# The second expert layer in units of 32 tokens, in plain fp32 with four column groups, each expert's weights loaded once

## The reference

```python
def moe(h, w_router, b_router, w1, w3, w2):
    N, D = h.shape                                   # second layer: 512, 1024
    scores = jax.nn.sigmoid(h @ w_router)            # 16 experts in 4 groups of 4
    ...                                              # best group, then its two best experts
    wts = wts / wts.sum(-1, keepdims=True)           # weights of the two
    ...                                              # tokens sorted by expert
    def expert_block(args):
        xb, e = args
        return (jax.nn.silu(xb @ w1[e]) * (xb @ w3[e])) @ w2[e]
    ...
    return jnp.zeros((N, D), h.dtype).at[tok_s].add(out[dest] * w_s[:, None])
```

## Time and profile before

| | us |
|---|---|
| median of three runs | 2587.99 |
| lowest, highest | 2586.57, 2590.0 |
| span of the profiled execution | 2585.1 |
| PE busy | 2436.7 (94%) |
| DVE busy | 1915.5 (74%) |
| ACT busy | 1327.3 (51%) |
| POOL busy | 298.1 (12%) |
| PE's share of the chain that ended last | 89% |

### The profile page before, as it was taken

The page is one execution under the profiler, slowest core; times in us unless marked ns, Lnnn a source line. Parts: engine busy times, 40 slices in busy tenths (PEclk is TensorE's granted clock), DMA queues, the critical chain, the costliest instruction groups (busy, mean ns, idle before and its releaser), DMA issues.

```text
span 2585.1 us, 30193 instructions
## 1 busy us (share of the span) xinstructions
PE 2436.7 (94%) x10883; PEld 1767.2 (68%) x10883; DVE 1915.5 (74%) x2100; ACT 1327.3 (51%) x1280; POOL 298.1 (12%) x330
## 2 busy tenths in 40 slices
PE   6999988996999999999979999999988999999995
PEld 3555534545888888888758887666446888888884
DVE  2899956446888888888857724776357888898887
ACT  3000104115777777777562234465116777777774
POOL 0534411220000000000110002110000000000002
PEclk8999999997999999999979999999988999999998
DMA  9110265439999999999951233125339999999994
GB/s 337 40 66 33 82 252 150 159 139 379 422 422 396 385 388 388 387 387 386 357 213 56 77 117 116 35 87 184 147 147 368 422 401 391 388 388 380 387 387 148
DMA packets 151272, 671.84 MB, mean 260 GB/s; under 512 B 24938, under 2 KB 34410, under 8 KB 94882
## 3 DMA queue, kind: packets, MB, share of 16 engines
q1 hardware_dynamic: 128562, 591.68, 58.9%
q0 software_dynamic: 20208, 74.98, 8.0%
q10 hardware_dynamic: 2432, 4.26, 0.5%
HBM read 612.59 MB, written 58.29 MB: 260 GB/s over the span
## 4 chain that ended last, share of the span: by engine, by line
PE 89%; DVE 3%; DMA 3%; ACT 2%; issue 1%; SPq 1%; POOL 1%; ACTq 0%; DVEq 0%; POOLq 0%
PE ps L826 85%; PE ps L1010 1%; PE ps L1016 1%; ACT arena L1303 1%; DMA arena<-in_w_in_ab_dram 1%; PE ps L914 1%; SPq L411 0%; DMA buf_d<-arena 0%; POOL arena L699 0%; DMA arena<-buf_d,slots 0%; DMA buf_d<-arena,slots 0%; PE ps L1272 0%; DVE arena L1754 0%; DMA arena<-buf_d 0%; DMA arena<-in_w_ada_dram 0%
## 5 line engine op out<-in xcount | busy, mean ns | idle before, releaser
L1864 DVE TENSOR_TENSOR wl<-wx,wh 128x2048 fp32r<-128x2048 f32 x432 | 969.2, 2286 | 49.2 <-ACT wh L1303 49.2
L1303 ACT ACTIVATE wh<-wx 128x2048 fp32r<-128x2048 f32 x432 | 819.4, 1915 | 160.0 <-PE ps L826 143.1
L826 PE MATMUL ps<-wh,xT 128*128 128x512 f32 x2304 | 736.5, 396 | 4.9 <-DVE xT L1881 4.9
L826 PE MATMUL ps<-arena 128*128 128x512 f32 (+5 forms) x2232 | 714.0, 492 | 14.9 <-ACT arena L1303 6.5
L826 PEld LDWEIGHTS ps<-arena 128*128 128x128 f32 (+1 forms) x2232 | 381.2, 188 | 322.4 <-issue 293.2
L826 PEld LDWEIGHTS ps<-wh,xT 128*128 128x128 f32 x2304 | 435.2, 189 | 105.8 <-DVE xT L1881 5.7
L826 PE MATMUL ps<-wl,xT 128*128 128x512 f32 x1152 | 455.1, 395 | 0.0
L826 PE MATMUL ps<-wh,gT 128*128 128x512 f32 x1152 | 378.2, 399 | 0.0
L1303 ACT ACTIVATE arena<-ps 128x512 f32<-128x512 f32 (+7 forms) x231 | 139.6, 619 | 449.3 <-PE ps L826 365.3
L826 PEld LDWEIGHTS ps<-wl,xT 128*128 128x128 f32 x1152 | 217.7, 189 | 47.2
L826 PEld LDWEIGHTS ps<-wh,gT 128*128 128x128 f32 x1152 | 216.8, 188 | 47.3
(11 more groups left out here) (255 smaller groups left out, 2262.9 us busy)
## 6 DMA issues: line engine op xcount, KB each, us to landing
wx<-in_w_dram SPq DMA_DIRECT2D x432, 1024.0 KB, 8.5
arena<-in_w_ada_dram SPq DMA_DIRECT2D x40, 1024.0 KB, 8.3
arena<-buf_d POOLq DMA_DIRECT2D x38, 512.0 KB, 10.7
buf_d<-arena POOLq DMA_DIRECT2D x36, 512.0 KB, 7.8
craw<-in_w_in_c_dram SPq DMA_DIRECT2D x8, 2048.0 KB, 8.6
buf_d<-arena POOLq DMA_DIRECT2D x1, 14848.0 KB, 57.4
arena<-in_w_in_ab_dram SPq DMA_DIRECT2D x8, 1024.0 KB, 12.6
arena<-in_w_out_ab_dram SPq DMA_DIRECT2D x4, 2048.0 KB, 8.0
```

The lines of the kernel that those rows point to most:

```text
L826: return pe.matmul(bank_ap, lhsT, rhs, start=first, stop=last)
L1303: return act.activation(out_, in_, f, **kw)
L1864: v.tensor_tensor(wl[:, g], wx[:, g], whs[g % NH].bitcast(F32), ALU.subtract).then_inc(m["low"], 1)
```

## The change

In the second layer, the buffer of 128-row blocks goes. DRAM gets `h_d` (each token's normalised row, stored by ACT) and `xi_d`, a list of token numbers with room for 768 entries for each expert. `scatter` writes 16-byte entries into `xi_d`. DVE builds a table `utab`: for each unit its expert (`U_E`), its first entry (`U_ROW`); for each expert the units before it (`U_BEF`); and the number of units (`U_N`).

A unit is up to 32 tokens of one expert. POOL reads the unit's 32 entries four times over into `uix` (128 numbers of 4 bytes) and gathers 128 quarter rows of 1 KB into `ux`, so the array's 128 partitions hold 4 quarters by 32 tokens. PE transposes that with two instructions. `sweep` then multiplies in plain fp32: for each of four groups and two slices it sends four products, one for each quarter of 256 output columns, to the four column groups of the array. Three sweeps make a unit: 96 matmuls. The product of gate and value moves from DVE to POOL. ACT stores the result.

The weights take two places. SP loads group `g` of expert `e` into `un_raw[g]` when the copy of expert `e-1` out of it is done. DVE copies it to the fixed place `un_w[g]` when the last unit of expert `e-1` has used that. There is no split into high and low parts, and each expert is loaded once.

```diff
@@ SP
+            def unit_weights(e, groups, later=False):
+                for g in groups:
+                    if later:
+                        sp.wait_ge(un["copied"], e * PAIRS + (g + 1 - PAIRS))
...
+                    sp.dma_start(un_raw[g].rearrange("p k n -> p (k n)").unsqueeze(1), src).then_inc(un["w"][g // 2], 16)
@@ POOL
+                def rows_of(u):
+                    r = pool.value_load(utab[0:1, bass.ds(U_ROW + u, 1)], min_val=0, max_val=NSLOT - UT)
+                    pool.dma_start(uix[:, 0:1], xi_rows[:, bass.ds(r, UT), :], allow_slow_non_contiguous=True).then_inc(un["ix"], 16)
+                def gather_x():
+                    pool.indirect_dma_start(ux, None, h_rows, bass.IndirectOffsetOnAxis(ap=uix[:, 0:1], axis=0)).then_inc(un["xg"], 16)
...
+                with pool.Fori(0, nu) as u:
+                    pool.wait_ge(un["xg"], u * 16 + 32)
+                    rows_of(u + 2)
+                    pool.wait_ge(un["turn"], u * 2 + 2)
+                    pool.wait_ge(un["ix"], u * 16 + 48)
+                    pool.wait_ge(un["hid"], u * 2 + 2)
+                    pool.tensor_tensor(ugg, us0, ugg, ALU.mult).then_inc(un["g"], 1)
+                    gather_x()
@@ PE
+                def sweep(bank, e12, g0, actsT, s):
+                    for g in range(4):
+                        pe.wait_ge(un["copied"], e12 + (g0 + g + 1))
+                        for i in range(2):
+                            for q in range(4):
+                                ins = mm(ps[32 * q:32 * q + 32, bank, 0:256], actsT[:, i * P + 32 * g:i * P + 32 * g + 32],
+                                         un_w[g0 + g][:, i, 256 * q:256 * q + 256], g + i == 0, g + i == 4)
+                        ins.then_inc(s, 1)
+                def place(u):
+                    return pe.value_load(utab[0:1, bass.ds(U_E + u, 1)], min_val=0, max_val=PAIRS * (NX - 1))
...
+                with pe.Fori(1, nu) as u:
+                    gate_up(u, place(u), False)
+                    down(u - 1, place(u - 1))
+                    turn_g(u)
+                down(nu - 1, place(nu - 1))
@@ ACT
+                        if n == 3:
+                            act.wait_ge(h_rdy, j + 1)
+                            act.dma_start(h_d[(t - CT) * P:(t - CT + 1) * P, :], hall[:, t, :]).then_inc(un["h"], 16)
...
+                with act.Fori(1, nu) as u:
+                    silu(u, False)
+                    up(u, False)
+                    turned_x(u + 1)
+                    out_y(u - 1)
+                    turned_g(u)
@@ DVE
+                with v.Fori(0, NX) as e:
+                    c = v.value_load(utab[0:1, bass.ds(U_BEF + e, 1)], min_val=0, max_val=UMAX)
+                    for g in range(PAIRS):
+                        v.wait_ge(un["w"][g // 2], e * 32 + 32)
+                        if g < 8:
+                            v.wait_ge(un["gu"], c * 8 + (g + 1))
+                        else:
+                            v.wait_ge(un["w2"], c * 4 + (g - 7))
+                        v.tensor_copy(un_w[g], un_raw[g]).then_inc(un["copied"], 1)
```

More of the change, by code:

```diff
@@ L58 @@
 FMAX = S // P - 1
+UT = 32
+CAP = S
+NSLOT = NX * CAP
+UMAX = 2 * S_LAT // UT + NX - 1
+U_E, U_ROW, U_BEF, U_N = 0, 64, 128, 144
 EPS = 1e-6
@@ L78 @@
 C_SEL = 600
-C_END = 696
+C_U = 696
+C_END = 698
+C_TOK = C_END + P + NX
 def i_mod32():
@@ L132, in program @@
     buf_v = buf_d.rearrange("(b p) d -> p b d", p=P)
+    h_d = dram("h_d", [S_LAT, D])
+    xi_d = dram("xi_d", [NSLOT, 4], I32)
     es = ExitStack()
@@ L215, in program @@
         ln_pe, ln_dv, ln_act = sems("ln_pe ln_dv ln_act")
[L217 to L221, removed]
+        moe = {s: sem(f"m0_{s}") for s in "used high low xg tx ab si g tg ye yst done".split()}
+        moe["w"] = [sem(f"m0_w{i}") for i in range(PAIRS // 2)]
+        un = {s: sem(f"un_{s}") for s in "gu w2 copied ix xg turn actsT hid g ye yst h".split()}
+        un["w"] = [sem(f"un_in{i}") for i in range(PAIRS // 2)]
         cw, hl_rdy, c_high, c_low, z_use = sems("cw hl_rdy c_high c_low z_use")
@@ L303, in program @@
         geff = at(50480, 2 * KE * NX + NX)
+        un_raw = [at(6144 + 2048 * UNIT_PLACE[g], 2, D) for g in range(PAIRS)]
+        un_w = [at(30720 + 2048 * g if g < 9 else 2048 * (g - 9), 2, D) for g in range(PAIRS)]
+        ux, uxT, us0, ugg, ugT, uy = (at(49152 + 256 * i, 256) for i in range(6))
+        uix = nc.alloc_sbuf_tensor_at("uix", [P, 2], I32, offset=base + 4 * 50688)[:]
+        tokf = at(50696, 4 * NT)
+        tok = nc.alloc_sbuf_tensor_at("tok", [P, NT, 4], I32, offset=base + 4 * 50720)[:]
+        utab = nc.alloc_sbuf_tensor_at("utab", [P, 192], I32, offset=base + 4 * 50744)[:]
+        u_th, u_tt, u_tr = at(48240, NX, NX), at(48496, 4, 32), at(48624, P)
+        h_rows = h_d.rearrange("s (c n) -> (s c) n", c=4)
+        y_rows = buf_d[0:UT * UMAX, :].rearrange("s (c n) -> c s n", c=4)
+        u_sk = at(50936, 2, NT - CT)
+        u_slots = nc.alloc_sbuf_tensor_at("u_slots", [P, 2, NT - CT], I32, offset=base + 4 * 50944)[:]
+        xi_rows = xi_d.rearrange("s (c o) -> c s o", o=1)
         def item_at(n):
@@ L580, in _ @@
             for n in range(16, 24):
-                sp.wait_ge(moe[0]["used"], nb * PAIRS + (n - 16 + 4))
+                sp.wait_ge(moe["used"], nb * PAIRS + (n - 16 + 4))
                 item_load(n)
-            sp.wait_ge(moe[0]["done"], 1)
+            sp.wait_ge(moe["done"], 1)
             chain(2)
@@ L652, in _ @@
             chain(3)
-            sp.wait_ge(moe[1]["xg"], 16)
-            await_stores(sp, 4)
-            expert_weights(1, 0, None, range(6, PAIRS))
+            units()
+            sp.wait_ge(un["copied"], NX * PAIRS)
             sp.wait_ge(u_st[1], stored(10, 1))
@@ L817, in _ @@
             scatter(1)
-            pool.wait_ge(u_mm, 40)
-            experts(1)
+            units()
             gather(4)
```

221 lines of the change are left out of this document (196 added, 25 removed).

## The result

The changed kernel takes 2602.35 us (median of four runs, 2602.12 to 2608.14) against 2588.24 for the kernel before on the same chip. The ratio is 1.0061, with a 95% interval from 1.0047 to 1.0075. It is slower by 0.6%. The forecast was 2575.

A forecast was written before the change was run, and what follows sets the result against it. PE was taken to bound the 602 us stage, with transfers nearly full. Changed stage: 573 plus 13 for GpSimd, 586; with +3 at the start, 2575 us. Range 2530 to 2625, likeliest case 2550 to 2592.

The forecast's parts named there:

- max(units x 12.3, 32.2): Second layer, per expert: the larger of PE's 12.3 us a unit and 32.2 us of loads; sum 597.3 us.
- the same two thirds: Share taken of the lead from loads starting one unit before a PE-bound expert's end: 24 us off 597.3, leaving 573.
- the 13 us for GpSimd: Added to the stage for POOL's product held by DVE's copy bursts: a third of the lower end of 34 to 60.
- Sets in four column groups: PE's sweeps: four matmuls run at once in 0.433 us a set, 24 sets or 10.4 us a unit, 32-wide loads hidden.
- The unit's price: PE's time for one unit: 10.4 + 0.44 + 0.6 + 0.85 = 12.3 us, bounds 11.4 and 13.2.
- the table read: PE's read at the unit loop's head, exposed once a unit because its queue is empty: 0.85 us.
- L = 32.2: Transfers per expert, weights at 422 GB/s plus gathers, results and small reads: 32.2 us, bounds 30.4 and 35.5.
- DVE's copy: DVE's 128x2048 weight copy to the fixed place: 1.28 us taken, 2.29 if slow.
- the rival at 2597 to 2640: POOL's product or gather held at full price by DVE's copies at changes of expert: 2597 to 2640 us, chance 0.22.
- late gathers: POOL's gathers landing too late for the next unit; part of the 2640 us upper case, chance 0.22 with held products.
- The clock: PE may fall to 1.2 GHz where it waits for landings; 1.73 us groups still fit 2.6 us intervals, so nothing charged.
- Start and end: Second layer's ends: list read and gather before the first turn add 3 us, bounds 0 and +7; the end 0.

The follow-up runs named there:

- e3: Changed kernel with POOL's product first, the next list read ahead into a second column, and the result store moved to POOL's queue: 2571.10 us, ratio 0.9943.
- e5: e3 with weight transfers from the second expert on cut to an eighth, the products using old weights for the rest: 2484.7 us, one run.
- e1: Changed kernel with POOL's product first and the next list read ahead through a second column of `uix`: 2599.28 us, ratio 1.0040.
- e8: e3 with the second layer's experts taken in the order 12 to 15, 0 to 11: 2552.39 us, ratio 0.9861.

## Why the prediction was wrong

The kernel became 14 us slower where 13 us faster was forecast. The time lies inside the stated range, but no case of the forecast had what brought it there.

**The step that failed** is the one that let an expert cost "about max(units x 12.3, 32.2)". It has two terms, PE and the loads. A third was missing: a unit can be no shorter than the longest ring of dependent transfers, 14 to 15 us here while weights load. In the forecast's own sum it changes nothing for the nine experts with one or two units (2 x 14.8 = 29.6, under 32.2). It makes 44.4, 59.2 and 74 us of three, four and five units: 660 in all, less a lead of 30 by the same two thirds, 630 in place of 573. The stage measured 616, against 586 forecast with the 13 us for GpSimd. The text came near the rings twice. It said that a gather "is issued about 2.3 us after the unit's gate sweep and has 12 us in all; it lands in 5.8", and looked no further than this one transfer. The list read, 3.4 us to landing by the earlier trace rows, was put on the path at the start only. The order of POOL's instructions, shown ahead of the prediction, had POOL's ring in full: the gather waits for the list, the list for the gather before, and the product stands behind both. Adding them with the landings of the earlier trace rows gives 5.8 + 3.4 + about 3 for issues and the product, 12.2 us: already level with the unit's 12.3. The one result store in flight was not priced at all; its nearest row is the 10.7 us of a 512 KB load. e3 shows what the rings cost: with POOL's ring opened and the store's shortened, the time falls by 31 us to 2571. That this is 4 us from the forecast is in part luck: 0.8 us too much for each unit and the 13 us for GpSimd stand against terms that were too small (see the end of this section).

**Sets in four column groups: right.** Gate and value are 16 sets in 7.11 us. Less the same 0.17 of tail that is 0.434 us a set, against 0.433 forecast from the 72 records of the earlier trace rows. The Trainium skill's 62 ns for a matmul with hardware decode off ("TensorE: Matmul & The Clock Gate", section on the 56 ns gap), counted for each record as in the prediction, would have needed 7.9 us for these 128 records. No run shows whether hardware decode is on here. The row has 7.11, over whole sweeps, so the queue filled ahead did not flatter the row of before.

**The unit's price: right in kind, 0.8 us too high.** 11.5 us against 12.3, inside its bounds of 11.4 and 13.2. From start to start the four parts of a unit are 7.04 + 0.44 + 3.59 + 0.44 = 11.51. The 24 sets are 10.41 of it, so the four transposes and the four changes of the array take 1.10, against 0.44 + 0.6 forecast. The split was off: each turn, two transposes, takes 0.44, twice the forecast's 0.11 for one, and the changes are left with 0.22. What was too much is the table read, 0.85: it is free while PE's queue is full. After a stall it may show: in the changed kernel PE sits idle for 0.91 us, put down to "issue", between the turn at 2114.58 and the sweep at 2115.99.

**Loads: nearly right.** 32.3 us an expert in the chain of e3, against L = 32.2; over twelve experts of e3, from DVE's first copy of expert 1 (1975.07) to that of expert 13 (2375.40), it is 33.4. In the changed kernel the mark set for the loads (DMA share of 0.95 or more with PE waiting for DVE's copies) was half met: the share is 1.02 from 1990 to 2100, but PE waits for DVE's copies only 11 us in the whole stage. A high DMA share alone did not tell what PE waited for.

**DVE's copy: right.** One row of the changed kernel by form, as in the earlier trace rows:

```profile
L2092 DVE COPY arena<-arena 128x2048 f32<-128x2048 f32 x192 | 231.4, 1268 | 363.1 <-PE ps L919 334.5 <-DMA arena<-in_w_dram 26.8 <-issue 1.8
```

1.27 us against 1.28, from the row with one input.

**GpSimd held by DVE's copies: wrong as a mechanism.** The +13 in the sum and the rival at 2597 to 2640 both rested on the earlier trace rows. The rival's time came about, the mechanism did not: POOL's product is 0.73 us in the median and 1.36 at most in the changed kernel, and with all copies kept e5 runs at 11.5 us a unit but for the two places named there. Its neighbour, "late gathers", was closer, but what made them late was the wait for lists and landings. The mark "unit starts above 14 us inside one expert (issue, reads or late gathers)" did catch it.

**The clock: charged at nothing, which was too little.** The first sweep in the windows above took 9.62 us at a mean granted clock of 0.73, the second 7.11 at 1.00. The 0.73 is a mean of the two levels: 0.50 (1.2 GHz) from 2086.50 to 2091.64, full speed (2.4 GHz) behind it. The first sweep followed a turn for which PE had waited 5.0 us, the second followed a sweep without such a stall. In the changed kernel 16 of the 41 sweeps of gate and value last 8.3 to 10.0 us in place of 7.11, about 31 us in all. How much of that lies on the path is open: while a ring binds, a slower sweep hides in it in part.

**Start and end.** +2.7 us against +3, and -1.0 against 0. But the second unit starts 22.7 us after the first, because POOL's second gather and third list come one after the other ahead of the first product; that belongs to the rings, and in e3 it is 11.2.

**What stays open.** With the measured 11.5 and 32.3 the forecast's own formula gives 9 x 32.3 + 4 x 34.5 + 2 x 46 + 57.5 = 578, less a lead of 23, 555 us; e3's stage, from 1958.64 to 2535.83, has 577. The trace of e3 splits the 22 us at 2385.76, where expert 13 begins. Ahead of it lie 427 us, where the formula has 417: the DMA share is 1.02 from 1990 to 2375, experts with three and four units included, so the lead hid more of PE's work than the formula let it, and the loads took 33.4 us in place of 32.3. Behind it lie 150 us, where the formula has 138, and the clock there is full: 7.9 us of this is that the last unit needs 19.4 us from its start to its result, not 11.5. The forecast had no term for that. Why the loads took longer over twelve experts, and why the store lands sooner from POOL's queue than from ACT's, is open.

## What to carry to other kernels

When a block of work is cut into smaller ones, list for each small block every transfer that must land before the next may be issued, follow each list round once, and compare its length with the block's compute time: the longest ring is a lower bound that no busy share shows. It costs only what it adds to the other bounds: here next to nothing while most experts had two units, and 25 us behind them. Price each landing at the load that the new kernel will have, not at its quiet value, and look at every buffer with one place. If two rings are about equally long, undoing one does nothing, so an edit without effect does not acquit its suspect: try both together.

## What the runs showed of the hardware

- A 128 KB result store from ACT's queue takes about 15 us to land (14.9 and 15.5 us in the changed kernel, 15.9 in e1) while the DMA engines move about 410 GB/s; from POOL's queue within 10.6 us in e3, 8.9 in the median in e8, and 4.3 in e5 with the loads cut to an eighth. The Trainium skill, "DMA: Bandwidth & Descriptors", section "Anatomy of one DMA — SWDGE (gpsimd) path", fits 2.0 us and the bytes at 436 GB/s for transfers of POOL's queue, which makes an estimate of 2.3 us for this size: no store that was timed here came near that under load.
- A read of 512 bytes as 128 numbers lands in 5.8 us (median, 5.3 to 8.5) beside full loads, in 2.5 when these are cut to an eighth.
- Four column groups with 32 stationary columns sustain a set of four plain fp32 matmuls of 256 columns every 0.434 us over sweeps of 128 records.
- A sweep behind a stall of PE of 5.0 us ran its first 5.1 us at a granted clock of 0.50 (1.2 GHz) and the rest at full speed, and lost 2.5 us.
- Beside twelve copies of DVE in a row (14.55 us), one POOL product took 1.7 us in place of 0.7 and the issue of one gather 2.0 in place of 1.0: POOL was held for about one copy, not for the burst (e5).
